# Seven half-size products in place of four blocks in the up projection of an MLP's last three groups

## The reference

```python
h = rms_norm(x, g[4])
f = jnp.square(jax.nn.relu(h @ w_up[l])) @ w_down[l]
x = x + rms_norm(f, g[5])
```

## Time and profile before

| | |
|---|---|
| median of 3 runs | 1481.72 us (1481.68 to 1481.8) |
| profiled execution | 1484.23 us, its span 1482.1 us |
| mean granted clock of TensorE | 0.998 of full speed |
| TensorE busy | 1463.4 us (99%), 7810 matmuls |
| VectorE, ScalarE, GpSimd busy | 896.6, 633.6, 381.8 us |
| DMA | 168.40 MB |

### The profile page before, as it was taken

The page is one execution under the profiler, slowest core; times in us unless marked ns, Lnnn a source line. Parts: engine busy times, 40 slices in busy tenths (PEclk is TensorE's granted clock), DMA queues, the critical chain, the costliest instruction groups (busy, mean ns, idle before and its releaser), DMA issues.

```text
span 1482.1 us, 19058 instructions
## 1 busy us (share of the span) xinstructions
PE 1463.4 (99%) x7810; PEld 1258.9 (85%) x7810; DVE 896.6 (60%) x1045; ACT 633.6 (43%) x877; POOL 381.8 (26%) x272
## 2 busy tenths in 40 slices
PE   9999999999999999999999999999999999999997
PEld 7978998889888888888898889988898988888886
DVE  6345554846467566575982464747466584757659
ACT  6335433634444343343562454325444342534344
POOL 2001820300171513315030028102002805151422
PEclk9999999999999999999999999999999999999999
DMA  8532132421324325152353233134203352423402
GB/s 285 179 94 94 58 128 85 160 96 57 114 86 142 114 94 162 57 170 100 114 192 121 65 97 124 58 113 170 86 29 114 115 169 86 141 87 119 137 29 100
DMA packets 83959, 168.40 MB, mean 114 GB/s; under 512 B 3744, under 2 KB 19872, under 8 KB 82848
## 3 DMA queue, kind: packets, MB, share of 16 engines
q1 hardware_dynamic: 82432, 164.90, 33.2%
q10 hardware_dynamic: 1440, 2.27, 0.4%
HBM read 160.87 MB, written 6.29 MB: 113 GB/s over the span
## 4 chain that ended last, share of the span: by engine, by line
PE 91%; DVE 4%; ACT 2%; issue 1%; DMA 1%; POOL 1%; POOLq 0%; SPq 0%; DVEq 0%; ACTq 0%
PE proj L748 25%; PE proj L750 25%; PE proj L749 25%; PE work L748 3%; PE work L750 3%; PE work L749 3%; PE work L777 2%; DVE w_lo L1492 1%; PE work L813 1%; PE work L823 1%; PE work L803 1%; ACT w_hi L1169 1%; PE work L905 1%; DMA w_raw<-in_w_up_dram 1%; PE work L884 0%
## 5 line engine op out<-in xcount | busy, mean ns | idle before, releaser
L1492 DVE TENSOR_TENSOR w_lo<-w_raw,w_hi 128x2048 fp32r<-128x2048 f32 (+1 forms) x103 | 235.6, 2287 | 253.4 <-ACT w_hi L1169 253.3
L748 PE MATMUL proj<-hT_hi,w_hi 128*128 128x512 f32 (+1 forms) x800 | 298.8, 374 | 2.1 <-DVE u L1528 2.1
L750 PE MATMUL proj<-hT_hi,w_lo 128*128 128x512 f32 (+1 forms) x800 | 297.7, 372 | 0.0
L749 PE MATMUL proj<-hT_lo,w_hi 128*128 128x512 f32 (+1 forms) x800 | 297.7, 372 | 0.0
L1169 ACT ACTIVATE w_hi<-w_raw 128x2048 fp32r<-128x2048 f32 (+1 forms) x103 | 185.2, 1798 | 235.1 <-PE proj L750 221.7
L748 PE MATMUL proj<-w_hi,hT_hi 128*128 128x512 f32 (+1 forms) x640 | 237.9, 372 | 1.1 <-DVE hT_lo L1684 1.1
L750 PE MATMUL proj<-w_hi,hT_lo 128*128 128x512 f32 (+1 forms) x640 | 232.2, 363 | 0.0
L749 PE MATMUL proj<-w_lo,hT_hi 128*128 128x512 f32 (+1 forms) x640 | 231.9, 362 | 0.0
L748 PEld LDWEIGHTS proj<-hT_hi,w_hi 128*128 128x128 f32 x800 | 150.7, 188 | 28.5 <-DVE w_lo L1492 2.7
L750 PEld LDWEIGHTS proj<-hT_hi,w_lo 128*128 128x128 f32 x800 | 150.7, 188 | 26.3
L749 PEld LDWEIGHTS proj<-hT_lo,w_hi 128*128 128x128 f32 x800 | 150.7, 188 | 25.9
(11 more groups left out here) (213 smaller groups left out, 2521.9 us busy)
## 6 DMA issues: line engine op xcount, KB each, us to landing
w_raw<-in_w_up_dram SPq DMA_DIRECT2D x32, 1024.0 KB, 5.6
w_more<-in_w_down_dram SPq DMA_DIRECT2D x24, 1024.0 KB, 5.1
w_raw<-in_w_in_dram SPq DMA_DIRECT2D x28, 768.0 KB, 4.4
w_raw<-in_x_wkv_dram SPq DMA_DIRECT2D x15, 1024.0 KB, 5.1
w_raw<-in_w_out_dram SPq DMA_DIRECT2D x8, 1024.0 KB, 5.2
w_raw<-in_x_wq_dram SPq DMA_DIRECT2D x8, 1024.0 KB, 5.0
w_raw<-in_x_wo_dram SPq DMA_DIRECT2D x8, 1024.0 KB, 5.0
w_hs<-in_w_down_dram SPq DMA_DIRECT2D x8, 1024.0 KB, 5.0
```

The lines of the kernel that those rows point to most:

```text
L748: nc.tensor.matmul(dst, l_hi, r_hi, start=first, stop=False, skip_group_check=more)
L749: nc.tensor.matmul(dst, l_hi, r_lo, start=False, stop=False, skip_group_check=more)
L750: return nc.tensor.matmul(dst, l_lo, r_hi, start=False, stop=last, skip_group_check=more)
L1492: nc.vector.tensor_tensor(w_lo[:, slot, :, 0:cols], w_raw[:, raw, :, 0:cols], w_hi[:, slot, :, 0:cols].bitcast(F32), ALU.subtract).then_in ...
```

## The change

**Products.** In groups 1 to 3 the up projection is now seven products too, p1, p2, p6, p5, p7, p3, p4 (`UPS`, `up_product`), each one 512 x 512 block of weights (a quadrant or a sum of quadrants) with 256 tokens moving: 4 tiles x 4 chunks x 3 matmuls of 256 columns. The token operands are quadrants of `hT` and three sums and one replaced quadrant, made and split once a layer during group 0 (`quadrant_sum_of`, `quadrant_split_hi`, `quadrant_split_lo`, `third_quadrant` on GpSimd). Products accumulate in two pairs of PSUM banks: p1, p6, p7, p4 in one, p2, p5, p3 in the other.

**Out of PSUM.** ScalarE copies p1, p1 + p6 and p5 into `u` (`up_copy`), VectorE adds the other pair's bank to it (`up_add`). The squared relu of `a11`, `a22` and `a12` is two passes on ScalarE (`up_square`), that of `a21` is on VectorE (`square_up_rest`).

**Weight sums.** A layer has seven phases with such sums, `PHASES = 7` (phase 0 the down projection of group 0, odd phases up, even ones down). The quadrants of a phase are a, b, c, d in five buffers (`phase_buffers`); the sums are all plus, with signs moved to the rows: c + d, f = c + a, then a + c and f + b. Only f is made by GpSimd, in four steps of 512 columns (`second_sum`); the other three are transfers from DRAM that add into the buffer (`add_by_dma`), two of 512 KB each, issued by GpSimd.

**Order.** The high and low halves of down rows now follow those of the weights of the same product. GpSimd's list is: the transfer into a, the difference of rows a5, the transfer into f, the transfer into the next phase's c, the next f.

```diff
+OPERAND = {"1": "a", "2": "b", "6": "f", "5": "c", "7": "a", "3": "f", "4": "d"}
+SUM_STEPS = 4
...
+            def up_product(l, g, name):
+                b = up_block(g, name)
+                slot = slot_of(l, b)
+                on_x = name in ("p1", "p6", "p7", "p4")
+                fresh = name in ("p1", "p2", "p5")
+                hi, lo = UP_ROWS[name]
+                pe.wait_ge(w_lo_done, nth(w_lo_done, l, b + 1))
+                if g == 1 and name in ("p6", "p5", "p7", "p4"):
+                    part = {"p6": "t2", "p5": "t1", "p7": "t3", "p4": "t4"}[name]
+                    pe.wait_ge(quadrant_lo, nth(quadrant_lo, l, QUADRANTS.index(part) + 1))
+                for i in range(2):
+                    if name in ("p1", "p2"):
+                        pe.wait_ge(added, nth(added, l, add_number(g - 1, "m3" if name == "p1" else "m4", i)))
+                    elif name in ("p6", "p7", "p3"):
+                        copied = {"p6": "p1", "p7": "p6", "p3": "p5"}[name]
+                        pe.wait_ge(up_copied, nth(up_copied, l, copy_number(g, copied, i)))
+                    else:
+                        read = {"p5": "p2", "p4": "p7"}[name]
+                        pe.wait_ge(up_added, nth(up_added, l, up_add_number(g, read, i)))
+                    for m in range(2 * i, 2 * i + 2):
+                        f = slice(m * P, (m + 1) * P)
+                        at = slice(m % 2 * (S // 2), (m % 2 + 1) * (S // 2))
+                        for k in range(BK):
+                            mm = three_passes(proj[:, (0 if on_x else 2) + i, at], w_hi[:, slot, k, f], w_lo[:, slot, k, f],
+                                              hi[:, k], lo[:, k], fresh and m % 2 == 0 and k == 0, k == BK - 1, more=True)
+                    mm.then_inc(tile_done, 1)
...
+            def up_copy(l, g, name):
+                bank = 2 if name == "p5" else 0
+                for i in range(2):
+                    act.wait_ge(tile_done, nth(tile_done, l, done(up_block(g, name), i)))
+                    if name == "p1":
+                        free = product_number(g - 1, "m6")
+                    elif name == "p6":
+                        free = product_number(g - 1, "m7")
+                    else:
+                        free = product_number(g - 1, "m3")
+                    act.wait_ge(a_lo_done, nth(a_lo_done, l, free + 1))
+                    nc.scalar.activation(UP_TARGET[name][:, 2 * i:2 * i + 2],
+                                         proj[:, bank + i].rearrange("p (m c) -> p m c", m=2), ACT.Copy).then_inc(up_copied, 1)
+            def up_square(l, g, part):
+                if part == "a12":
+                    act.wait_ge(a_lo_done, nth(a_lo_done, l, product_number(g - 1, "m4") + 1))
+                    for i in range(2):
+                        act.wait_ge(tile_done, nth(tile_done, l, done(up_block(g, "p4"), i)))
+                        nc.scalar.activation(a12[:, 2 * i:2 * i + 2], proj[:, i].rearrange("p (m c) -> p m c", m=2), ACT.Relu,
+                                             scale=-1.0).then_inc(rectified, 1)
+                else:
+                    act.wait_ge(up_added, nth(up_added, l, up_add_number(g, {"a11": "p2", "a22": "p7"}[part], 1)))
+                    nc.scalar.activation({"a11": a11, "a22": a22}[part], {"a11": a11, "a22": a22}[part], ACT.Relu,
+                                         scale=-1.0 if part == "a22" else 1.0).then_inc(rectified, 1)
+                whole = {"a11": a11, "a22": a22, "a12": a12}[part]
+                act.wait_ge(rectified, nth(rectified, l, rectified_number(g, part, 1 if part == "a12" else 0)))
+                nc.scalar.activation(whole, whole, ACT.Square).then_inc(squared, 1)
...
+            def later_up(l, g):
+                up_copy(l, g, "p1")
+                product_hi(l, g, "p6")
+                product_hi(l, g, "p5")
+                up_square(l, g, "a11")
...
```

On ScalarE the rest of `later_up`, and on VectorE `first_up`, `later_up` and the start of `down`:

```diff
+                product_hi(l, g, "p3")
+                up_copy(l, g, "p5")
                 rows_hi(l, g, "m1")
+                product_hi(l, g, "p4")
+                up_square(l, g, "a22")
                 product_hi(l, g, "m1")
                 rows_hi(l, g, "m5")
-                for m in range(4, 8):
-                    relu_up(l, g, m)
                 product_hi(l, g, "m5")
+                up_square(l, g, "a12")
...
+            def first_up(l):
...
+                square_up(l, 4)
+                quadrant_sum_of(l, "t4")
+                square_up(l, 5)
+                quadrant_split_lo(l, "t2")
+                square_up(l, 6)
+                square_up(l, 7)
+                rows_lo(l, 0, "m5")
+                product_lo(l, 0, "m5")
+                late_sum(l, 0, "m6")
...
+                product_lo(l, g, "p6")
+                if g == 1:
+                    quadrant_split_lo(l, "t4")
+                up_add(l, g, "p2")
+                product_lo(l, g, "p5")
+                product_lo(l, g, "p7")
+                product_lo(l, g, "p3")
+                rows_lo(l, g, "m1")
+                up_add(l, g, "p7")
+                product_lo(l, g, "p4")
+                if g == GROUPS - 1 and l < DEPTH - 1:
+                    for t in range(MT):
+                        norm_mem(l, "memk", t)
+                up_add(l, g, "p3")
+                square_up_rest(l, g)
+                product_lo(l, g, "m1")
+                rows_lo(l, g, "m5")
+                product_lo(l, g, "m5")
+                late_sum(l, g, "m6")
...
+                add_both(l, g, "m1")
+                product_lo(l, g, "m6")
+                rows_lo(l, g, "m6")
+                late_sum(l, g, "m7")
+                product_lo(l, g, "m2")
+                rows_lo(l, g, "m2")
+                if last:
+                    gather(l, "c22")
+                add_both(l, g, "m6")
+                product_lo(l, g, "m7")
+                rows_lo(l, g, "m7")
+                if last:
+                    gather(l, "c21")
+                late_sum(l, g, "m4")
```

On GpSimd:

```diff
+            def add_by_dma(l, p, q, more):
+                into = weights_in(BUFFERS[p][q])
+                if q == "c":
+                    loaded(l, p, "c")
+                elif q == "a":
+                    pool.wait_ge(t_made, nth(t_made, l, SUM_STEPS * (p + 1)))
+                    pool.wait_ge(w_lo_done, nth(w_lo_done, l, block_of(p, "1") + 1))
+                else:
+                    pool.wait_ge(w_lo_done, nth(w_lo_done, l, block_of(p, "6") + 1))
+                for h in range(2):
+                    k = slice(h * BK // 2, (h + 1) * BK // 2)
+                    nc.gpsimd.dma_start(into[:, k], quarter_of(l, p, more, k), accum_op=ALU.add).then_inc(dma_added[q], 16)
...
+            def second_sum(l, p):
+                c, a, f = (weights_in(BUFFERS[p][q]) for q in "caf")
+                pool.wait_ge(dma_added["c"], nth(dma_added["c"], l, 32 * (p + 1)))
+                loaded(l, p, "a")
+                if p == 0:
                     pool.wait_ge(turned_lo, nth(turned_lo, l, 2 * TURNED["n3", T - 1] + 2))
+                elif p % 2:
+                    pool.wait_ge(a_lo_done, nth(a_lo_done, l, product_number((p + 1) // 2 - 1, "m4") + 1))
                 else:
-                    pool.wait_ge(w_lo_done, nth(w_lo_done, l, group_block(g, 0) + 1))
-                for k in halves:
-                    nc.gpsimd.tensor_tensor(b22[:, k], b12[:, k], b22[:, k], ALU.add).then_inc(t_made, 1)
-                loaded(3)
-                for h, k in enumerate(halves):
-                    made(h + 1)
-                    nc.gpsimd.tensor_tensor(s2[:, k], b22[:, k], b11[:, k], ALU.subtract).then_inc(t_made, 1)
-                made(4)
-                for k in halves:
-                    nc.gpsimd.tensor_tensor(b12[:, k], b11[:, k], b12[:, k], ALU.subtract).then_inc(t_made, 1)
+                    pool.wait_ge(w_lo_done, nth(w_lo_done, l, block_of(p - 1, "7") + 1))
+                for k in range(SUM_STEPS):
+                    nc.gpsimd.tensor_tensor(f[:, k], c[:, k], a[:, k], ALU.add).then_inc(t_made, 1)
+            def rows_difference(l, g):
...
+                add_by_dma(l, 0, "c", "d")
+                second_sum(l, 0)
+                third_quadrant(l)
+                rows_difference(l, 0)
+                add_by_dma(l, 0, "a", "c")
+                for p in range(PHASES):
+                    if p:
+                        add_by_dma(l, p, "a", "c")
+                        if p % 2 == 0:
+                            rows_difference(l, p // 2)
+                    add_by_dma(l, p, "f", "b")
+                    if p < PHASES - 1:
+                        add_by_dma(l, p + 1, "c", "d")
+                        second_sum(l, p + 1)
```

More of the change, by code:

```diff
@@ L99, in raw_at, with phase_of, phase_buffers @@
-    slot = (i + g) % WSLOTS
-    earlier = sum(KB if slot == h % WSLOTS else KB + 1 for h in range(g))
-    return slot, HEAD_BLOCKS // WSLOTS + earlier + i // WSLOTS
+    assert b >= BLOCKS
+    return (b - BLOCKS) % WSLOTS, RAWS // WSLOTS
```

(37 more changed lines are left out.)

567 lines of the change are left out of this document (340 added, 227 removed).

## The result

The changed kernel takes **1518.62 us** (median of 4 runs, 1515.85 to 1520.53) against 1481.76 (1481.68 to 1482.72): 36.9 us slower, a ratio of 1.0246 with a 95% interval of 1.0228 to 1.0264. Forecast were 1495 and a range up to 1522. The profiled span is 1517.8 us against 1482.1.

The account below looks back on a forecast made before the run. TensorE was taken as the bound, so only less work there saves time. 6 x (-3.1 + 1.4 + 0.4 + 0.7) = -3.6, 12 D = +12, group 0 +1.5 and last groups +3.5 gave +13.4 us: 1495, range 1480 to 1522.

Parts of the forecast that it names:

- the up products: Groups 1 to 3: seven products of 5.77 us replace four up blocks, 3.1 us saved per later group, -18.8 us.
- A: Later groups: m5 waits for a5, queued on Pool behind two adding transfers awaiting m1's low half; 1.4 + 2D a group.
- the last group of layer 0: Two memory norms, 1.28 each, stand ahead of m1's low half: +2.5 us.
- slow adding transfers: Rival: sums by adding transfers come late, deciding from 11.4 us per MB; time 1506 to 1550, chance 0.2.
- the wait of 2.15 us: Layer 0, TensorE waiting for the first square behind a low half that met Pool: mostly won back, -1.9 us.
- D: Time of one transfer issue on Pool, taken as 1.0 us; 12 D gives +12 us in all.
- C: Down phases: rows split behind their own weights, a wait of 0.33 at every second product, 0.7 in all eight phases.
- B: Behind m5's start: squares of a12, the second difference and m1's adds delay m6's halves, 0.4 us a later group.
- Group 0: m5's high half behind last relu and rows, 1.7 each for two, less 1.9; quadrant sums at nothing: +1.5 us.
- the gathers: Gathers ahead of the low halves of m7 and m3: 0.5 us in each last group, 1.0 together.
- Issue is free: Rival: Pool hands issues off, D near 0 (decides below 0.13): +1.4 us, 1483; chance 0.14.
- Faster: Rival: A falls away as a5 comes by 39.8, or m5's weights are split first: -7, 1475; chance 0.15.

Follow-up runs that it names:

- experiment 4: Kernel before, with only the high and low halves of down rows moved behind those of the same product's weights: 1492.26 us, ratio 1.0070.
- experiment 2: Changed kernel plus five float32 matmuls of zeros on TensorE ahead of m5 in groups 1 to 3: 1507.25 us, 1.0172.
- Experiment 8: Changed kernel with a5 ahead of the adding transfers (1490.95 us), and all 84 adding transfers made plain copies: 1484.02 us, 1.0015.
- run 12: Run 9 plus group 0's squares ahead of the fourth quadrant sum, memory norms in the last down phase, m5's weights ahead of its rows: 1472.93 us, 0.9941.
- run 5: Changed kernel with a5 ahead of the adding transfers, rows' halves of m6, m2, m7, m3, m4 one product ahead, m7's sum ahead of m6's weights: 1502.39 us.
- run 9: Changed kernel with a5 ahead of the adding transfers, and rows' halves of m2, m7, m3 and m4 ahead of their weights' halves: 1480.42 us, 0.9995.

## Why the prediction was wrong

**Right:** the direction; the up products (3.3 us saved a group, 3.1 forecast; no wait for PSUM copies, as forecast); the place, the cause and the releasers of A; no waits put down to an adding transfer.

**Right by luck:** the last group of layer 0, +2.6 for +2.5. Its two memory norms took 4.55 us beside GpSimd's sum, not 2.5, and some 2 us of that were covered, where none were taken to be. The time of 1518.6 lies under the upper end of the range, 1522, but that end stood for slow adding transfers, which TensorE did not wait for. And the wait of 2.15 us, credited with -1.9, is gone, but that cannot be credited to the change: experiment 4 and the second layer of the kernel before do not have it either, and the profiled execution that has it took 1484.2 where the median is 1481.7.

```profile
707.42 4.55 DVE L1908 SCALAR_TENSOR_TENSOR mems<-mems,mem_rstd,gains 128x1024 f32<-128x1024 f32 x2
```

**The step that failed is the price of A**, "1.4 + 2D", 3.4 us a group. It priced a wait on TensorE by its length. The six waits lost 26.2 us by their length (4.1, 4.1, 3.5, 4.8, 4.9, 4.7), 20.4 were forecast. In each, D was 1.23 for 1.0 and GpSimd started 0.55 and not 0.1 behind the low half. In layer 1 m1's low half also ended 0.7 us later, behind squares of a21 that ran beside GpSimd's sum, a kind of collision that the prediction took at nothing. Layer 0 and layer 1:

```profile
623.30 1.49 DVE L1835 SCALAR_TENSOR_TENSOR u<-u 128x512 f32<-128x512 f32 x2
...
1285.40 2.20 DVE L1835 SCALAR_TENSOR_TENSOR u<-u 128x512 f32<-128x512 f32 x2
```

The granted clock fell at each of the six waits, within it or up to 1 us behind it, and was back 3 to 6 us behind its end. That stood nowhere in the sum: 12.5 us by the steps of m5's matmuls, 11.4 by experiment 2.

**C was mis-sized**: 0.7 a phase, measured 1.3 (experiment 4), since the pause is 0.42 and there are three. Over the six later phases 7.5 for 4.2; B's 0.4 was not seen.

**Group 0**: forecast +1.5 in two layers, measured +5.8. "Early in the 22 us of the second up blocks; I take nothing" was wrong for the fourth sum and the low half behind it, which stand between the last squares. VectorE in the changed kernel, and TensorE's wait for it:

```profile
442.52 4.48 DVE L1739 TENSOR_TENSOR w_lo<-w_raw,w_hi 128x2048 fp32r<-128x2048 f32 x1
...
457.02 1.28 DVE L1765 TENSOR_TENSOR hT_lo_sum<-work,t_sum 128x512 f32<-128x512 f32 x2
458.22 0.68 DVE L1816 SCALAR_TENSOR_TENSOR u<-proj,u 128x512 f32<-128x512 f32 x1
458.82 1.22 DVE L1783 SCALAR_TENSOR_TENSOR t_lo<-t_sum,t_hi 128x1024 fp32r<-128x1024 f32 x1
459.95 1.29 DVE L1816 SCALAR_TENSOR_TENSOR u<-proj,u 128x512 f32<-128x512 f32 x2
...
460.78 0.47 PE L893 MATMUL proj<-w_hi,a_hi 128*128 128x512 f32 x1 [2.46 <-DVE u L1816]
```

1.28 and 1.22 us ahead of the last squares, and 4.48 for a low half that ran beside GpSimd's quadrant sum: from the last up matmul to m1's first are 2.8 us (1.4 in layer 1), and in layer 0 slow matmuls follow here as well (granted clock 0.50 from 461.9 to 465.3).

The stretching beside GpSimd that the prediction reads from its rows is the same by single instructions: of GpSimd's pair of sums at 433.82 in the kernel before, the first takes 2.41 us (2.39 for one alone at 426.63); VectorE's low half, started at 434.16, ends at 438.37, 2.1 behind that sum's end at 436.23; the second sum, started at 436.18, takes 4.45 and ends 2.3 behind the low half.

The sum with measured terms: up -19.8; later down phases 26.2 + 7.5 + 12.5 = 46.2 (measured 46.3), and 0.7 behind the last matmul, whose cause stays open; group 0 +5.8; last up +2.6; rest +0.1; 35.7 us. Of the gap of some 22 us to the forecast of +13.4, the clock is 12.5, A's length 5.8, group 0 4.3, C 3.3, the end 0.7, less B 2.4, the up products 1.0 and the gathers 1.0.

**The rivals.** *Slow adding transfers* did not decide: the MB, in two issues, is there a median of 9.5 us behind the first, under the 11.4 from which the rival was to decide. Experiment 8 is 6.9 us faster all the same, some 5 us without the lost start, by landing and issue together. *Issue is free* was wrong (1.23 us). *Faster* named its own condition, "m5's weights to be split before a5's rows"; with that order and a5 ahead of the transfers (run 12) 1473 us were measured for the 1475 worked out.

## What to carry to other kernels

Where TensorE is at 99%, price a wait with the slow matmuls that may follow it: here six waits of 3.5 to 4.9 us (4.4 in the mean) cost 2.1 us more each, at a granted clock of 0.50. In a list ordered by hand, ask of every instruction that is put first whether what stands behind it needs it: two issues ahead of a5 cost 27.7 us, a5's rows ahead of m5's weights 4.6, m6's rows and m7's sum ahead of m6's weights 22 (run 5 against run 9), where the shorter up phases save 20. After one wait is removed, look for the next before judging a second edit.

## What the hardware showed that was not expected

- An adding transfer issued from GpSimd holds that engine for 1.2 us in 52 cases of 84 (changed kernel), else 1.3 to 2.2, a plain one for 0.72 (SyncE's queue: 0.37). Twelve of the 84 adding ones stand 3.9 to 6.6 us longer at "issue"; with `dynamic_dma_scratch_size` at 3072, or as plain transfers, none does.
- The adding transfer of 512 KB lands in a median of 8.0 us, the plain one in 4.9 (the 36 of `w_down`).
- From one matmul's start to the next: 0.9 to 2.1 us in the MLPs of these runs left the granted clock at 1.00, the six of 3.8 to 5.1 us in the changed kernel each came with 0.50. Between, it went both ways: around 2.3 us (714.33 in the changed kernel) it fell, after 2.47, 2.70 and even 3.46 us (457.84 in run 9, 636.63 and 707.75 in run 5) it did not.
- The first matmul after such a short pause (0.52 from start to start) takes 0.31 to the next and not 0.23, 0.08 of the 0.42 that such a pause costs over two products.
